# The opening of a diffusion backbone in two halves of its feature blocks

## The reference, cut to what matters

```python
def rms_norm(x, g):
    xf = x.astype(jnp.float32)
    y = xf * lax.rsqrt(jnp.mean(xf * xf, axis=-1, keepdims=True) + EPS)
    return (y * g.astype(jnp.float32)).astype(x.dtype)

def swiglu(h, wg, wu, wd):
    return (jax.nn.silu(h @ wg) * (h @ wu)) @ wd
```

## Time and profile before

| | before |
|---|---|
| runs, median (range) | 2163.85 us (2163.36 to 2164.53) |
| the profiled execution, its own time | 2162.38 us |
| its span, first to last instruction | 2160.6 us |
| PE busy in the span | 2114.4 us (98%) |
| DVE busy | 1481.3 us (69%) |
| ACT busy | 1014.0 us (47%) |
| POOL busy | 615.3 us (28%) |
| mean granted TensorE clock | 0.997 of full speed |

### The profile page before, as it was taken

How to read it: one execution, slowest core, us unless ns; L and a number is a source line. 1 busy time by engine, 2 the same in 40 slices (tenths; PEclk the granted TensorE clock), 3 DMA queues, 4 the chain that set the end, 5 groups by cost and what they waited for, 6 DMA issues and landing times.

```text
span 2160.6 us, 31674 instructions
## 1 busy us (share of the span) xinstructions
PE 2114.4 (98%) x11845; PEld 1776.3 (82%) x11845; DVE 1481.3 (69%) x2074; ACT 1014.0 (47%) x1589; POOL 615.3 (28%) x615
## 2 busy tenths in 40 slices
PE   7999999999999999999999999999999999999998
PEld 4878788987766778988888898888889887888997
DVE  4898898875576456877777775445457868776555
ACT  4544445554455543554344553222245556745444
POOL 1566666402000027344444420000013201261000
PEclk9999999999999999999999999999999999999999
DMA  9487686623333354655556465545545445576564
GB/s 309 133 233 200 171 217 173 190 78 97 94 114 89 90 174 134 185 167 161 156 159 177 138 185 156 150 141 157 155 127 157 118 125 154 150 207 178 184 185 137
DMA packets 471963, 340.61 MB, mean 158 GB/s; under 512 B 13226, under 2 KB 437654, under 8 KB 471686
## 3 DMA queue, kind: packets, MB, share of 16 engines
q1 hardware_dynamic: 441312, 238.06, 38.7%
q0 software_dynamic: 29056, 96.35, 15.9%
q10 hardware_dynamic: 1446, 4.20, 0.5%
HBM read 326.98 MB, written 12.36 MB: 157 GB/s over the span
## 4 chain that ended last, share of the span: by engine, by line
PE 84%; DVE 8%; issue 4%; ACT 3%; DMA 1%; POOL 0%; SPq 0%; DVEq 0%; ACTq 0%; POOLq 0%
PE bank L832 18%; PE bank L833 18%; PE bank L837 18%; PE bank L900 4%; PE bank L910 4%; PE bank L901 3%; DVE w_lo L801 3%; PE bank L984 2%; PE bank L985 2%; PE bank L990 2%; PE bank L1337 1%; PE bank L1313 1%; PE bank L1106 1%; PE bank L1105 1%; PE bank L1112 1%
## 5 line engine op out<-in xcount | busy, mean ns | idle before, releaser
L801 DVE TENSOR_TENSOR w_lo<-raw,w_hi 128x1024 fp32r<-128x1024 f32 (+1 forms) x442 | 580.9, 1316 | 472.8 <-PE bank L837 258.9
L791 ACT ACTIVATE w_hi<-raw 128x1024 fp32r<-128x1024 f32 (+1 forms) x442 | 461.6, 1044 | 590.8 <-PE bank L833 291.1
L832 PE MATMUL bank<-h_hi,w_hi 128*128 128x512 f32 (+1 forms) x1728 | 597.5, 358 | 3.0 <-DVE X L2028 1.5
L833 PE MATMUL bank<-h_lo,w_hi 128*128 128x512 f32 (+1 forms) x1728 | 592.0, 355 | 0.0
L832 PEld LDWEIGHTS bank<-h_hi,w_hi 128*128 128x128 f32 x1728 | 326.5, 189 | 52.6 <-issue 4.4
L837 PE MATMUL bank<-h_hi,w_lo 128*128 128x512 f32 (+1 forms) x1728 | 367.1, 355 | 0.0
L833 PEld LDWEIGHTS bank<-h_lo,w_hi 128*128 128x128 f32 x1728 | 326.6, 189 | 46.3 <-issue 1.0
L837 PEld LDWEIGHTS bank<-h_hi,w_lo 128*128 128x128 f32 x1728 | 291.5, 189 | 45.5
L832 PE MATMUL bank<-inner_hi,w_hi 128*128 128x256 f32 (+1 forms) x654 | 205.5, 336 | 2.5 <-DVE X L2028 2.5
L833 PE MATMUL bank<-inner_lo,w_hi 128*128 128x256 f32 (+1 forms) x654 | 204.4, 334 | 0.0
L2452 POOL DMA_DIRECT2D wm<-in_w_mod_dram x128 | 92.6, 724 | 361.9 <-DVE gstage L2000 158.0
(11 more groups left out here) (300 smaller groups left out, 3448.8 us busy)
## 6 DMA issues: line engine op xcount, KB each, us to landing
wm<-in_w_mod_dram POOLq DMA_DIRECT2D x128, 512.0 KB, 4.4
raw<-in_w_in_dram SPq DMA_DIRECT2D x108, 512.0 KB, 4.1
raw<-in_ffn_w_down_dram SPq DMA_DIRECT2D x94, 512.0 KB, 4.1
raw<-in_ffn_w_gate_dram SPq DMA_DIRECT2D x88, 512.0 KB, 4.5
raw<-in_ffn_w_up_dram SPq DMA_DIRECT2D x88, 512.0 KB, 4.2
raw<-in_w_out_dram SPq DMA_DIRECT2D x24, 512.0 KB, 3.9
raw<-in_ffn_w_down_dram SPq DMA_DIRECT2D x24, 384.0 KB, 3.9
raw<-in_w_branch_dram SPq DMA_DIRECT2D x16, 512.0 KB, 4.3
```

The costliest lines, as they stand in the source:

```text
L791: act.activation(w_hi[w_slot[n]][:, 0:unit.rows, :], raw[unit.slot][:, 0:unit.rows, :], ACT.Copy).then_inc(hi_made, 1)
L801: dve.tensor_tensor(w_lo[w_slot[n]][:, 0:unit.rows, :], raw[unit.slot][:, 0:unit.rows, :], w_hi[w_slot[n]][:, 0:unit.rows, :].bitcast(F32) ...
L832: pe.matmul(psum, w_hi[s][:, k, :], hi, start=(k == 0), stop=False)
L833: mm = pe.matmul(psum, w_hi[s][:, k, :], lo, start=False, stop=False)
```

## The change

It writes the opening of layer 0 in another order.

- **Tokens first.** Before any modulation, PE turns two blocks of one stream at a time (`turn_tokens(m)`, m = 0 to 3 latent, 4 to 7 context). DVE, no longer ACT, copies them to `X`; ACT squares them; DVE adds the squares, each stream by itself; `sum_tokens` sums them.
- **Halves.** The modulation groups are reordered (`MOD_ORDER`), so that groups 0 and 1 hold shift and scale of blocks 0 to 3. `opening_vectors(0)` makes their vectors, the norm runs over blocks 0 to 3 in both streams, and `opening_quad` runs four units over these blocks, 512 columns at a time. The last eight pieces stand between its steps, groups 2 and 3 are turned, `opening_vectors(1)` follows, then the norm and the products of blocks 4 to 7, where the four units go round together and no longer one behind the other.
- **Loads.** SP issues 8 pieces, the four units of the first quad, then the other 8 pieces; these no longer pass through `raw`. The second group of small parameters (`pack2`) is issued by POOL, not by ACT. The copies to `skip_w` stand behind the norm.
- `run_on` is gone.

The diff, cut to its core:

```diff
+MOD_ORDER = (0, DC, DC // 2, DC + DC // 2)
@@ SP: the loads of the opening
                     for j in range(MOD_FIRST):
-                        if j >= 14:
-                            sp.wait_ge(unit_done, j - 14 + 8 + 1)
+                        if j == MOD_FIRST // 2:
+                            for p in range(4):
+                                load(first["up", 0, 1, 0] + p, 0, (0, 0), ((0, DC), columns((ffn1_w_gate, ffn1_w_up)[p % 2], 0, p // 2 * P)))
+                        if 10 <= j < 13:
+                            sp.wait_ge(unit_done, j - 6 + 1)
+                        if j == 13:
+                            pe_start.wait(sp, ("x", 7))
@@ PE: the first quad
+            def opening_quad(u0):
+                for step in range(HALF + 3):
+                    for which in range(4):
+                        if 0 <= step - which < HALF:
+                            opening_step(u0 + which, which, step - which)
+                    if step in LATE_PIECES:
+                        i, j = LATE_PIECES[step]
+                        modulation(i, j)
+                        modulation(i, j + 1)
+                    if step == LATE_TURN:
+                        turn_modulation(2)
+                turn_modulation(3)
+                for k in range(HALF, DC):
+                    for which in range(4):
+                        opening_step(u0 + which, which, k)
@@ PE: the start
-                    for i in range(MOD_FIRST // 4):
-                        for j in range(4):
-                            modulation(i, j)
...
-                    turn_modulation(MOD_FIRST // 4 - 1)
-                    run_on(8)
+                    for m in range(4):
+                        turn_tokens(m)
+                    modulation(0, 0)
+                    sum_tokens(0)
+                    turn_tokens(4)
+                    turn_tokens(5)
...
+                    modulation(0, 3)
+                    turn_packs()
+                    modulation(1, 0)
+                    turn_modulation(0)
+                    modulation(1, 1)
+                    sum_tokens(1)
+                    modulation(1, 2)
+                    modulation(1, 3)
+                    turn_modulation(1)
@@ ACT
+                    for m in range(4):
+                        square_tokens_start(m)
+                    act.activation(early_root[:, 6:7], eps_col[:, 0:1], ACT.Sqrt)
+                    norm_root((0, 1), 0)
+                    for m in range(4, 8):
+                        square_tokens_start(m)
+                    copy_modulation(0)
+                    norm_root((0, 1), 1)
@@ DVE
+                    for k in range(HALF):
+                        for st in range(2):
+                            norm_scale((0, 1), k, st)
+                        for st in range(2):
+                            norm_lo((0, 1), k, st)
+                        split_lo(dve, k)
+                    opening_vectors(1)
```

## The result

The changed kernel takes 2176.01 us (median of five rounds, 2173.20 to 2179.02) against 2163.85 (2162.41 to 2165.36) of the kernel before in the same rounds. The ratio is 1.0054, with a 95% interval of 1.0040 to 1.0068: 12.2 us slower. The forecast was 6.2 us slower, with a range that ended at 2173.5, so the measured time lies outside it. The sign is right, the size half of what it should be.

The account below looks back on a forecast made before the run. PE fills most of the run, but DVE's chain from ACT's split of unit 4 decides the opening. 2.5 for that split plus 3.7 for the clock made 6.2: 2168.6 own time, plus 1.47 to the median, 2170.0; range 2163.0 to 2173.5.

Parts of the forecast that it names:

- The frame: Opening: DVE's chain decides, starting at ACT's split of unit 4 once unit 0 has used its high parts, 62.68 before.
- Rival B: DVE's chain gives way, PE's own order and the quad's end (67.3 against 69.23) decide; 2162 to 2163.5; chance 0.10.
- Rival D: The early start carries through, the first half ending 5 to 7 earlier than 53.3; under 2159.5; chance 0.05.
- Steps 1 to 3: Timetable of tokens, first half, second half: first product 33.3, last turn 53.3, block 4 at 56.35, split of unit 4 at 65.2.
- +2.5 later: ACT's split of unit 4 at 65.2 against 62.68, since unit 0 ends only 2 us ahead of the quad.
- Rival A: The clock pauses are not paid, or only partly at the third; 2166.4 to 2168; chance 0.17.
- step 5: Loads and copies in the opening: `pack2` on POOL's queue, `skip_w` copies, late pieces and POOL's loads cost nothing.
- Step 4: Slow clock behind three PE pauses in the opening: 1.0, 1.0 and 1.7, together 3.7 us.
- the first pause: PE idle 4.3 from 20.1 to 24.45, at the turn of group 0; clock loss behind it taken as 1.0.
- the second pause: PE idle 3.0 and two shorter pauses, 30.2 to 36.3, around the first product; clock loss behind it taken as 1.0.
- Rival C: Token stage longer than counted, late parameters or slow first turns and sum; up to 3 more, 2171 to 2173.5; chance 0.08.
- my discount: First two PE pauses in the opening taken at 1.0 each instead of 1.7; the full rule would give 1.4 more.

Follow-up runs that it names:

- e3: Kernel before, with stream 1 of the first quad done by all four units together, block by block, instead of in two pairs; 2169.73 us, ratio 1.0024.
- e7: Kernel before, with unit 1 running eight steps behind unit 0 instead of two in stream 1 of the first quad; 2161.55 us, ratio 0.9989.
- e1: Changed kernel with 31 idle multiplications, results unread, put into PE's pauses of the opening; 2167.10 us, ratio 1.0018.
- e8: Changed kernel with idle multiplications only around the turn of group 1 and in the first two steps of the first half; 2173.56 us, ratio 1.0042.
- e4: Kernel before without its eight idle multiplications ahead of the first product; 2163.58 us, ratio 0.9997.
- e9: Changed kernel with idle multiplications, diagonal second half, ACT's group 0 copy before squares 6 and 7, and stream 1's root before group 1's copy; 2164.02 us, ratio 1.0005.
- e2: Changed kernel with the second half of the first quad in diagonal order, units one block apart, instead of four units per block; 2169.88 us, ratio 1.0029.

## Why the prediction was wrong, and what of it held

**The frame held.** That the chain starts with ACT's split of unit 4 and that this split hangs on unit 0 was the step on which everything rested. e3 and e7 move that one moment in both directions, by +5.79 and -1.62, and the medians move by +5.7 and -2.2. The 6.5 us of lead had another source than the steps 2, 4 and 6 (see e3), which changes no sum. The distance from the split to the first multiplication of the down product was 79.96 and is 80.77. Rival B, PE's own order, is out: in e3 PE could have begun unit 4 at 69.55 (it starts at 71.49 and has waited 1.94 for ACT), against 69.23 in the kernel before, and the time is 5.7 higher. Rival D fell as said, with the last turn at 59.35.

**Steps 1 to 3, the timetable, held.** Run without slow clock (e1) it gave 32.75, 53.35, 56.28 and 65.41 for 33.3, 53.3, 56.35 and 65.2. That 53.3 was met to 0.05 is partly luck: the first product came 0.55 early and the first half took 0.6 longer. The term "+2.5 later" for the lost lead is 2.73. Rival A was the case of no clock loss, at 2166.4 to 2168: e1 makes that case true and takes 2167.1. `pack2` on POOL's queue, the late pieces and the loads cost nothing, as step 5 says: PE never waited for one of them.

**Step 4, the clock, is the step that failed.** Its mechanism was there, its size was not: it put 3.7 on the slow clock, and the runs showed 7.55. By differences between after and e1 (their moments are in the table):

| stretch | lost to the clock | the prediction had |
|---|---|---|
| up to the first product | 36.42 - 32.75 = 3.67 | 1.0, behind the first pause |
| first product to last turn done | 22.93 - 20.60 = 2.33 | 1.0, behind the second pause |
| pause ahead of block 4 | 0.0 | 0 |
| first product of block 4 to the split | 10.68 - 9.13 = 1.55 | 1.7 |

The last row is the one stretch for which the trace of before had a true likeness, a pause of 2.37 and dense work behind it, and it is right within 0.15. That is partly luck: in e8 the same pause with the same work behind it lost 11.76 - 9.13 = 2.63. The other two failed for three reasons. First, I counted the pauses that the new order makes at the turn of group 0 and later, and left out what lies ahead of them, though my own timetable contained it: PE has little to do while DVE and ACT do three rounds of 2.02. The row at 14.69 shows it, 2.76 of idle time and a sum of 1.96 instead of the 1.03 of e1. Slower still than counted were the very first turns (3.65 for 2.13, at 6.60). By the time of the turn of group 0, where the first counted pause stands, 26.05 - 23.83 = 2.22 of the 3.67 were lost: some 0.8 by the first turns, the rest by the sum and the turns behind it. Behind the counted pauses 1.45 and 2.33 were lost, against 1.0 and 1.0. Second, the loss was bounded by 1.7 for each pause because that is what the place of before had lost. But the clock does not always come back so soon: in after it stays at 0.50 from 36 to 44 although PE has no wait behind 39.37, and in e8 from 59 to 65 with PE at work throughout. A price per pause was the wrong form. Third, I gave the first two pauses a discount since DVE would be late anyway. That idea is right and e4 shows it: 5.1 us of missing clock for 0.28. But it was used where it doesn't hold: in the token stage of the new order every turn, sum and copy is a link of one chain through PE, ACT and DVE, so a slow sum is late by its whole length. Rival C had "the first turns at the low clock and the sum behind them too" in it, with a chance of 0.08, and it belonged into the forecast.

The Trainium skill, page "TensorE: Matmul & The Clock Gate", section "Terms", gives the price of slow clock as the throttled time times (1 - K/N). That is my 13.7 us in the first 160 us of after, and it is neither what after lost (7.55 at the split and 0.7 behind it) nor what e4 lost (0.28 for 5.1). By these runs it is an upper bound for the time in which the granted clock reads low; the first turns, slow at a reading of 1.00, come on top. What the prediction quoted from the Trainium skill, the same page's "Part 1: The HAM clock gate", that by that rule alone all three pauses would be paid, was nearer than my discount (5.1 for 3.7), and still too low, since it was applied to three pauses at 1.7 each.

**Behind the split** the prediction had nothing. The addition to X at 267.04 is 11.01 later for a split 10.28 later, so 0.73 arises there. Unit 6 waits 4.10 as forecast, and 90 to 96 run at 0.50 behind it. Pieces of the chain of waits of after (start, us, what):

```profile
90.16 0.96 ACT w_hi L813
91.12 0.14 issue
91.25 0.77 PE bank L854
...
152.26 1.63 PE bank L871 x7
153.89 0.23 PE bank L874
```

In the earlier trace rows the chain reaches the down product through DVE's `inner_lo` at 141.90. In after it goes over to PE at unit 6 and arrives on PE, without a wait: the slow half rate has made PE the late one, by 0.8 (80.77 for 79.96). In e1 the wait at unit 6 is nearly the same, 4.07, but 1.7 us of clock are missing behind it instead of 3.4, the distance is 79.98, and the addition is 2.77 later for a split 2.73 later. e3 and e8 also have a wait of 4.1 there and 1.7 missing, and lose nothing either (additions 5.78 and 9.01 later for splits 5.79 and 8.96 later). That fits, but no run fills that wait alone, so this part is read from traces and not shown by an edit.

The sum as it should have stood: 2.7 for the order, 7.6 for the clock up to the split, 0.7 behind it, 0.4 at 262.87 and 0.3 outside the span. That is 11.7; the two profiled executions differ by 11.9, the medians by 12.2. That the last tenths agree is luck: at the addition at 1949.54 of before the two traces are 10.80 apart, at the end of the span 11.6.

## What to carry to other kernels

Where a chain of single results leads through an engine that rests between its links, don't price the slow clock as one fixed loss per pause, since the same pause lost 1.55 here and 2.63 there. List every pause of the new timetable, the start and those one thinks of as hidden included, and run the kernel once with the pauses filled: the difference is the price. Look for the event that starts the chain behind a stage, not for the end of the stage: giving one unit of a quad its result early, at the cost of the others, was worth what it moved, in both directions, and one number in the kernel before (e7) gains 2.2 us, where the new opening in its best form (e9) gains nothing that can be measured. A slow clock costs next to nothing while another engine is late (0.28 for 5.1 in e4), so before filling a pause ask who waits for the work behind it.

## What the runs showed of the hardware that I had not expected

- **The low clock can last while the array works.** In after it stayed at 0.50 from 36 to 44 us with PE busy 6.36 of 8 us, with no wait behind 39.37, and in e8 from 59 to 65 us with PE at work from 59.88 on. In e1 the same stretch with 41 in place of 17 multiplications has 1.00.
- **Useless work can pay.** 31 idle multiplications of 0.47 us each (the row at 53.21 is six of them, two records each, in 2.84) took the time from 2176.0 to 2167.1.
- **Where the clock falls differs between executions.** The clock around 30 us was low in after and full in e2, with the same instructions up to there. The second half lost 1.55 to the clock in after and 2.63 in e8, behind the same pause and with the same work. A single profile of a kernel with pauses can't be read to better than 2 us in such a stretch.
- **A slow sum is slow in full, a slow product may be free.** The sum of stream 0 took 1.96 for 1.03 and everything behind it was late; ten microseconds of products at 0.50 in e4 cost 0.28.
- **Slow work need not show in the granted clock.** The sixteen records of the first turns took 3.65 in after and 2.13 in e1, where idle multiplications ran ahead of them, and the granted clock reads 1.00 in both.
